# Seven local changes around attention, the output slabs and the embedding gate of a two-layer transformer in one kernel

## The reference, cut to what matters

```python
def hybrid_mixer(u, ...):
    z = u @ w_in                                   # u is rmsnorm(h)
    ...                                            # q, k, v, f_logit: slices of z
    y_attn = forgetting_attention(q, k, v, f_logit) @ w_attn_out
    y_conv = conformer_conv(z[..., C0:GA0], conv_w, conv_b, g_conv) @ w_conv_out
    merged = sigmoid(z[..., GA0:GC0]) * y_attn + sigmoid(z[..., GC0:]) * y_conv
    return merged @ w_out

for i in range(2):
    h = h + 0.5 * swiglu(rmsnorm(h, g_ff1[i]), ...)
    h = h + hybrid_mixer(rmsnorm(h, g_mix[i]), ...)
    h = h + 0.5 * swiglu(rmsnorm(h, g_ff2[i]), ...)
    gate = sigmoid(rmsnorm(h, g_ple[i]) @ w_ple_gate[i])
    h = h + gate * (p[i] @ w_ple_proj[i])
```

## Time and profile before

| | us |
|---|---|
| median of 3 runs | 3079.8 |
| lowest and highest of them | 3076.36, 3082.9 |
| the profiled execution, its own time | 3081.73 |
| its span in the trace | 3079.8 |
| TensorE matmuls busy | 2966.8 (96% of the span) |
| VectorE, ScalarE, GpSimd busy | 2100.2, 1419.6, 483.1 |

### The profile page before, as it was taken

One profiled execution on the slowest core, in us unless ns is written; L12 is line 12 of the kernel. 1 busy time (PEld: TensorE's weight loads), 2 busy tenths in 40 slices (PEclk: granted clock), 3 DMA queues, 4 the chain that ended last, 5 costly groups with the idle time before them and its releaser, 6 DMA issues.

```text
span 3079.8 us, 51785 instructions
## 1 busy us (share of the span) xinstructions
PE 2966.8 (96%) x19012; PEld 2552.3 (83%) x19012; DVE 2100.2 (68%) x3101; ACT 1419.6 (46%) x2295; POOL 483.1 (16%) x392
## 2 busy tenths in 40 slices
PE   7999999999999999999999999999999999999998
PEld 4788888887889988777789987799887777899886
DVE  5666665445599845887699844899547886789535
ACT  3655565443356522334456622566323334466422
POOL 0213223066510011000200012100110000200012
PEclk9999999999999999999999999999999999999998
DMA  6122020223223322222222232223222222233322
GB/s 251 50 53 46 25 66 20 63 79 106 101 84 109 106 91 84 76 69 76 103 94 98 100 110 89 90 101 103 99 86 82 76 69 82 96 109 106 103 97 70
DMA packets 94911, 270.91 MB, mean 88 GB/s; under 512 B 35440, under 2 KB 36592, under 8 KB 93424
## 3 DMA queue, kind: packets, MB, share of 16 engines
q1 hardware_dynamic: 94016, 267.89, 26.3%
q0 software_dynamic: 320, 1.05, 0.1%
q10 hardware_dynamic: 432, 0.02, 0.0%
HBM read 263.68 MB, written 5.24 MB: 87 GB/s over the span
## 4 chain that ended last, share of the span: by engine, by line
PE 83%; DVE 8%; ACT 4%; issue 3%; SPq 2%; DMA 1%; ACTq 0%; DVEq 0%
PE bank L149 15%; PE bank L151 15%; PE bank L150 15%; PE bank L2028 8%; PE bank L2029 8%; PE bank L2030 8%; PE bank L1600 1%; ACT weights_hi L137 1%; SPq L666 1%; DVE weights_lo L142 1%; PE bank L1614 1%; PE bank L1666 1%; PE bank L2526 1%; PE bank L1669 1%; PE bank L2537 1%
## 5 line engine op out<-in xcount | busy, mean ns | idle before, releaser
L142 DVE TENSOR_TENSOR weights_lo<-weights_raw,weights_hi 128x1024 fp32r<-128x1024 f32 (+2 forms) x258 | 393.3, 1524 | 335.3 <-ACT weights_hi L137 331.2
L137 ACT ACTIVATE weights_hi<-weights_raw 128x1024 fp32r<-128x1024 f32 (+2 forms) x250 | 284.9, 1140 | 441.7 <-PE bank L151 433.1
L149 PE MATMUL bank<-x_hi,weights_hi 128*128 128x512 f32 x832 | 338.8, 407 | 9.9 <-DVE x_lo L1916 3.6
L151 PE MATMUL bank<-x_hi,weights_lo 128*128 128x512 f32 x832 | 327.4, 394 | 0.0
L150 PE MATMUL bank<-x_lo,weights_hi 128*128 128x512 f32 x832 | 326.2, 392 | 0.0
L2028 PE MATMUL bank<-sum_hi,block_hi 128*128 128x256 f32 x960 | 272.4, 284 | 3.7 <-ACT bank L2180 3.7
L150 PE MATMUL bank<-hidden_lo,weights_hi 128*128 128x512 f32 x704 | 273.9, 389 | 0.0
L149 PE MATMUL bank<-hidden_hi,weights_hi 128*128 128x512 f32 x704 | 273.9, 389 | 0.0
L151 PE MATMUL bank<-hidden_hi,weights_lo 128*128 128x512 f32 x704 | 273.9, 389 | 0.0
L2029 PE MATMUL bank<-sum_lo,block_hi 128*128 128x256 f32 x960 | 271.9, 283 | 0.0
L2030 PE MATMUL bank<-sum_hi,block_lo 128*128 128x256 f32 x960 | 270.7, 282 | 0.0
(11 more groups left out here) (457 smaller groups left out, 7472.2 us busy)
## 6 DMA issues: line engine op xcount, KB each, us to landing
raw_pair<-w_ff1in SPq DMA_DIRECT2D x42, 1024.0 KB, 4.9
raw_pair<-w_ff2in SPq DMA_DIRECT2D x42, 1024.0 KB, 4.9
weights_raw<-w_mix SPq DMA_DIRECT2D x72, 512.0 KB, 3.3
weights_raw<-w_ff1out SPq DMA_DIRECT2D x32, 704.0 KB, 4.0
weights_raw<-w_ff2out SPq DMA_DIRECT2D x32, 704.0 KB, 4.1
weights_raw<-w_tail SPq DMA_DIRECT2D x42, 512.0 KB, 3.3
mod_weights<-w_mod SPq DMA_DIRECT2D x6, 2048.0 KB, 16.4
weights_raw<-w_dn SPq DMA_DIRECT2D x24, 512.0 KB, 3.5
```

The source lines that it names most:

```text
L137: nc.scalar.activation(K.wh[:, slot, 0:cols], K.raw[:, slot, 0:cols], ACT.Copy).then_inc(S.wh_ready, 1)
L142: nc.vector.tensor_tensor(K.wl[:, slot, 0:cols], K.raw[:, slot, 0:cols], K.wh[:, slot, 0:cols].bitcast(F32), ALU.subtract).then_inc(S.raw_ ...
L149: nc.tensor.matmul(out, K.wh[:, slot, a:b], xh, start=start, stop=False)
L151: return nc.tensor.matmul(out, K.wl[:, slot, a:b], xh, start=False, stop=stop)
```

## The change

1. TensorE writes the first slab of stage c to bank 3 (VectorE reads it there), so that slab 2 finds bank 0 free and waits only for its own weights; slab 3 waits as before.
2. The cumulative forget sum is moved behind the eviction of the first slab of stage at, and that eviction ahead of the `split_lo` of slab 2.
3. `logits(0)` is moved ahead of the four taps that stood before it.
4. ScalarE makes `conved_hi` ahead of the `split_hi` of slab `s1 + 29`, which is the second slab of stage am, and TensorE waits for the convolved tiles one by one.
5. Output slabs 0 and 1 are interleaved: seven K tiles of slab 0, four of slab 1, the last of slab 0, the last four of slab 1.
6. At output slabs 0 to 5 ScalarE and VectorE split the weights of slab m + 2 before they make the parts of x tile m; at slabs 6 and 7 the order stays.
7. The first slab of stage ple goes to banks 4 and 6, and slab 2 no longer waits for its eviction.

```diff
-    def pe_project(pe, s, v, slot, q=None):
+    def pe_project(pe, s, v, slot, bank=None):
...
-            last = mm3(pb[slot][:, :], slot, k, xgh[:, k, :], xgl[:, k, :], k == 0, k == 7)
+            last = mm3(pb[slot if bank is None else bank][:, :], slot, k, xgh[:, k, :], xgl[:, k, :], k == 0, k == 7)
...
-        pe_project(pe, s0, v0, 0)
+        pe_project(pe, s0, v0, 0, 3)
         pe_sum_squares(pe, q)
         pe_project(pe, s0 + 1, v0 + 1, 1)
-        with pe.Fori(1, 4) as i:
+        pe_project(pe, s0 + 2, v0 + 1, 0)
+        pe_project(pe, s0 + 3, v0 + 3, 1)
+        with pe.Fori(2, 4) as i:
...
-            if first:
-                pe.wait_ge(S.cv_ready, 4 * (l + 1))
             for k in range(4):
+                if first:
+                    pe.wait_ge(S.cv_ready, 4 * l + k + 1)
                 last = mm3(pb[2 + slot][:, :], slot, 4 + k, K.cv_h[:, k, :], K.cv_l[:, k, :], k == 0, k == 3)
...
-        wo(0, 0, True)
-        wo(1, 1, False)
+        pe.wait_ge(S.raw_read, s4 + 1 + CREDIT)
+        pe.wait_ge(S.evac, v4 + 1)
+        for k in range(7):
+            pe.wait_ge(S.mg_ready, 8 * l + k + 1)
+            wo_tile(0, k)
+        pe.wait_ge(S.raw_read, s4 + 2 + CREDIT)
+        pe.wait_ge(S.evac, v4 + 2)
+        for k in range(4):
+            wo_tile(1, k)
+        pe.wait_ge(S.mg_ready, 8 * l + 8)
+        wo_tile(0, 7).then_inc(S.slab_done, 1)
+        for k in range(4, 8):
+            last = wo_tile(1, k)
+        last.then_inc(S.slab_done, 1)
...
-        split_hi(act, s1 + 29, 1, 1024)
         for t in range(4):
             act.wait_ge(S.cs_ready, 4 * l + t + 1)
             nc.scalar.activation(K.cv_h[:, t, :], K.cy[:, t, :], ACT.Copy).then_inc(S.cvh_ready, 1)
+        split_hi(act, s1 + 29, 1, 1024)
...
-        with act.Fori(0, 4) as i:
+        with act.Fori(0, 3) as i:
             for slot in range(2):
                 m = 2 * i + slot
+                split_hi(act, s4 + m + 2, slot, 1024)
                 act_gain(act, q + 1, m, v4 + m)
-                split_hi(act, s4 + m + 2, slot, 1024)
                 plain_x(act, q + 1, m)
...
-            nc.vector.tensor_tensor(K.glu[:, i, 30:542], pb[0][:, :], rstd[:, :], ALU.mult).then_inc(S.evac, 1)
+            nc.vector.tensor_tensor(K.glu[:, i, 30:542], pb[3 if first else 0][:, :], rstd[:, :], ALU.mult).then_inc(S.evac, 1)
...
+        dve.wait_ge(S.slab_done, s1 + 1 + CREDIT)
+        mixed_out(0)
+        dve.wait_ge(S.fln_ready, l + 1)
...
+        split_lo(dve, s1 + 2, 0, 1024)
         taps(4)
         slab_out(1)
         taps(4)
         slab_out(2)
+        logits(0)
         taps(4)
-        logits(0)
...
-        with dve.Fori(0, 4) as i:
+        with dve.Fori(0, 3) as i:
...
+                split_lo(dve, s4 + m + 2, slot, 1024)
                 dve_gain(dve, q + 1, m)
-                split_lo(dve, s4 + m + 2, slot, 1024)
...
-        tile(0, 0, True)
+
+        tile(0, 0, True, at=4)
         pe_sum_squares(pe, q)
         tile(1, 1, False)
-        with pe.Fori(1, 4) as i:
+        tile(2, 0, False, v0 + 2)
+        tile(3, 1, False)
+        with pe.Fori(2, 4) as i:
```

More of the change, by code:

```diff
@@ L2601, in mix_pe, with wo_tile, wo @@
         s4, v4 = K.slab(l, "wo"), K.evic(l, "wo")
-        def wo(m, slot, first):
+        def wo_tile(slot, k):
+            return mm3(pb[slot][:, :], slot, k, K.mg_h[:, k, :], K.mg_l[:, k, :], k == 0, k == 7)
+        def wo(m, slot):
             pe.wait_ge(S.raw_read, s4 + m + 1 + CREDIT)
@@ L2606, in wo @@
             for k in range(8):
-                if first:
-                    pe.wait_ge(S.mg_ready, 8 * l + k + 1)
-                last = mm3(pb[slot][:, :], slot, k, K.mg_h[:, k, :], K.mg_l[:, k, :], k == 0, k == 7)
+                last = wo_tile(slot, k)
             last.then_inc(S.slab_done, 1)
-        wo(0, 0, True)
-        wo(1, 1, False)
+        pe.wait_ge(S.raw_read, s4 + 1 + CREDIT)
[12 more added lines that the diff above has]
+        last.then_inc(S.slab_done, 1)
         with pe.Fori(1, 4) as i:
             for slot in range(2):
-                wo(2 * i + slot, slot, False)
+                wo(2 * i + slot, slot)
     def mix_act(act, l):
@@ L2727, in mix_act @@
         s4, v4 = K.slab(l, "wo"), K.evic(l, "wo")
-        with act.Fori(0, 4) as i:
+        with act.Fori(0, 3) as i:
             for slot in range(2):
                 m = 2 * i + slot
+                split_hi(act, s4 + m + 2, slot, 1024)
                 act_gain(act, q + 1, m, v4 + m)
-                split_hi(act, s4 + m + 2, slot, 1024)
                 plain_x(act, q + 1, m)
+        for m in (6, 7):
+            act_gain(act, q + 1, m, v4 + m)
+            split_hi(act, s4 + m + 2, m % 2, 1024)
+            plain_x(act, q + 1, m)
     def mix_dve(dve, l):
@@ L2787, in mix_dve, with mixed_out @@
             glu(i, False)
[L2788 to L2794, removed]
         s1, v1 = K.slab(l, "at"), K.evic(l, "at")
-        def slab_out(t):
-            split_lo(dve, s1 + t + 2, t % 2, 1024)
+        def mixed_out(t):
             kind, i = mixer_slab(t)
@@ L2809, in slab_out @@
             ins.then_inc(S.evac, 1)
+        def slab_out(t):
+            split_lo(dve, s1 + t + 2, t % 2, 1024)
+            mixed_out(t)
         def logits(n):
@@ L2833, in attended @@
                 .then_inc(S.ao_ready, 1)
-        slab_out(0)
+        dve.wait_ge(S.slab_done, s1 + 1 + CREDIT)
+        mixed_out(0)
+        dve.wait_ge(S.fln_ready, l + 1)
+        chain.link(nc.vector.tensor_tensor(K.fx[R, :], K.fx[R, :], K.fe[R, :], ALU.subtract))
+        chain.link(nc.vector.tensor_tensor_scan(K.fc[R, :], K.onerow[R, :], K.fx[R, :], 0.0, ALU.mult, ALU.add))
+        chain.link(nc.vector.tensor_copy(K.fch[R, :], K.fc[R, :]))
+        nc.vector.tensor_tensor(K.fcl[R, :], K.fc[R, :], K.fch[R, :].bitcast(F32), ALU.subtract).then_inc(S.cm_ready, 1)
+        chain.leave(LAYERS, FCHAIN)
+        hold(dve, S)
+        split_lo(dve, s1 + 2, 0, 1024)
         taps(4)
@@ L2895, in mix_dve @@
                 nc.vector.tensor_tensor(h[:, m, :], pb[slot][:, :], h[:, m, :], ALU.add).then_inc(S.evac, 1)
+                split_lo(dve, s4 + m + 2, slot, 1024)
                 dve_gain(dve, q + 1, m)
-                split_lo(dve, s4 + m + 2, slot, 1024)
+        for m in (6, 7):
+            dve.wait_ge(S.slab_done, s4 + m + 1 + CREDIT)
+            nc.vector.tensor_tensor(h[:, m, :], pb[m % 2][:, :], h[:, m, :], ALU.add).then_inc(S.evac, 1)
+            dve_gain(dve, q + 1, m)
+            split_lo(dve, s4 + m + 2, m % 2, 1024)
     def mix_pool(pool, l):
@@ L2927, in ple_pe, with tile @@
         s0, v0 = K.slab(l, "ple"), K.evic(l, "ple")
-        def tile(m, slot, first):
+        def tile(m, slot, first, freed=None, at=0):
             pe.wait_ge(S.raw_read, s0 + m + 1 + CREDIT)
-            pe.wait_ge(S.evac, v0 + m + 1)
+            pe.wait_ge(S.evac, v0 + m + 1 if freed is None else freed)
             if first:
@@ L3008, in tile @@
                 dve_rstd(dve, q, v0)
-            scaled(m, slot)
-            gated(m, slot)
+            scaled(m, slot, 4 if first else 0)
+            gated(m, slot, 4 if first else 0)
         tile(0, 0, True)
```

14 lines of the change are left out of this document (6 added, 8 removed).

## The result

The changed kernel took 3059.15 us (median of 4 runs, 3055.95 to 3059.49) beside 3081.1 us for the kernel before (4 runs): a ratio of 0.9929, 95% interval 0.9912 to 0.9946. That is 22 us less where 18.5 were forecast; the time lies inside the range of 3055 to 3068. The profiled execution took 3058.96 us, with a span of 3057.0.

A forecast was written before the change was run, and what follows sets the result against it. TensorE, busy nearly the whole span, was taken as the bound, so its stops set the gain. Layers' 7.5 and 7.8 us gave 15.3, plus 3.2 for the clock: 18.5, so 3061.3 against the median; range 3055 to 3068.

The forecast's parts named there:

- Edit 5's net of 1.34: Output slabs: interleaving with weights first removes a 2.26 us wait but adds 0.92 at slab 2, per layer.
- the squares get ahead of `weights_lo` of slab 2: Output slab 2: GpSimd's squares start at 1505.15, just ahead of `weights_lo`, which waits and ends at 1507.3.
- wait 0.52 for 0.65: Output slab 2: TensorE was forecast to stop 0.65 us for its weights, 0.92 charged with the restart.
- The third rival's counter-argument: Against new waits at output slab 2 and am (4.9 us less gain, chance 0.12): GpSimd's work starts after VectorE's weights request.
- The x part was taken at 0.7: Output slabs: VectorE's x part assumed as long as `h`, 0.7 us, in a slab total of 5.5 beside 5.4.
- the smaller of two numbers: Convolved tiles and stage am: TensorE's wait frees 1.81 us, the earlier merge loop 1.70; 1.70 was taken.
- 2.19 forecast: Stage ple, slab 2: the wait for the eviction vanishes, 1.92 + 0.27 = 2.19 us per layer.
- 0.70 for 0.60: Attention slab 2: with the forget sum moved, TensorE was forecast to go 0.60 us earlier, not the whole 1.11.
- 0.65 for 0.44: First turn: with `logits` ahead of the taps, `probs` was forecast to start 0.44 us earlier, about 1.5 of wait staying.
- the prediction moved `probs` by 0.32: First turn: `probs` starts when the taps end, moved by 0.28 of `logits` and its read-out, to about 1267.56.
- Two stretches of half rate: Layer 2, behind `merged_lo` and in ple: half-rate clock goes with the vanishing waits, 2 x 1.6 = 3.2 us.
- the one behind `probs` I leave, since 1.5 us of its wait stays: Behind `probs` of layer 1: the half-rate stretch was expected to remain, so no gain was counted.

The follow-up runs named there:

- squares_later: Changed kernel with GpSimd's squares of output slabs 0 to 5 held until the weights of slab m + 2 are split; output slabs 43.61 / 43.63 us, not 44.4.
- gain_first: Changed kernel with x tile parts again ahead of the weights at all output slabs, interleaving kept; output slabs took 46.24 / 46.30 us.
- tiles_only: Changed kernel with ScalarE's old order of `weights_hi` ahead of `conved_hi`, TensorE's tile by tile waits kept; first am to first output matmul 47.83 us.
- act_only: Changed kernel with TensorE waiting for all four convolved tiles at once, ScalarE's new order kept; first am to first output matmul 46.01 / 46.02 us.
- no_interleave: Changed kernel with output slabs 0 and 1 one after the other, weights still split first; output slabs 45.70 us in layer 1, 47.32 in layer 2.
- no_ple: Changed kernel with the bank change of stage ple undone; second feed-forward output to last slab matmul of layer 2 took 178.69 us, not 174.79.
- weights_before_sigmoids: Changed kernel with ScalarE making the weights ahead of the sigmoids in stage am; first am to first output matmul 43.52 us in both layers.

## Why the prediction was right, and where its sizes were off

**Edits 1, 4, 5 with 6, and 7** came within 0.2 us a layer of their terms. Edit 5's net of 1.34 rested on one step that could have gone either way, that the squares get ahead of `weights_lo` of slab 2: it went as worked out (wait 0.52 for 0.65; `weights_lo` 1.97 long), squares_later shows that it was GpSimd, and gain_first that without edit 6 nothing would be left. The third rival's counter-argument, that each unit of GpSimd's work starts after VectorE's request, doesn't fit this working: the squares stood 0.10 ahead in it and stand 0.15 ahead in the trace. The x part was taken at 0.7 and takes 1.77 at ten of 16 slabs (0.75 before), since it now starts while `square_sum` runs; it still ends inside the 5.4 us of a slab, so that this cost nothing.

**Edit 4** was said to be worth the smaller of two numbers, TensorE's wait and what the loop of merges gains by an earlier `gates`. tiles_only shows the first freed and nothing won, act_only the second alone and all of it won. `gates` starts 3.60 us behind the first am matmul, and not 5.43, which is where 1.8 rather than 1.7 comes from.

**Edit 7** gave 2.2 in layer 2 (2.19 forecast) and 2.0 in layer 1, for the longer wait at the first x tiles shown above; the prediction charged nothing there.

**Edit 2** gave 0.70 for 0.60: TensorE started 0.05 us behind the end of `weights_lo`, where it had started 0.15 behind `queries`.

**Edit 3** gave 0.65 for 0.44. The term that was mis-sized is what `logits` costs when it stands first. In the changed kernel:

```profile
1263.54 0.28 DVE L2836 CUSTOM_DVE_ANT_0 logits<-forget_rows,bank 128x128 f32<-128x128 f32 x1
1263.74 0.08 DVE L2836 DVE_READ_ACCUMULATOR2_ANT negmax<- 128x1 f32 x1
1263.74 2.73 DVE L2775 SCALAR_TENSOR_TENSOR conv_out<-glu,conv_taps,conv_out 128x512 f32<-128x512 f32 x4
1266.39 0.15 DVE L2842 RECIPROCAL rowinv<-rowsum 128x1 f32<-128x1 f32 x1
```

The taps start 0.20 behind the start of `logits`, where the prediction moved `probs` by 0.32 for it (1267.24 to 1267.56), and `probs` starts 2.65 behind the start of the taps, not 2.73: operations of VectorE overlap by 0.08 at a seam, which I had charged in full. Together 0.20 of the 0.21.

**The clock.** Two stretches of half rate were forecast to go with their waits, and they did (the output slabs and ple of layer 2, 3.2 us; no_interleave and no_ple bring one back each, 1.6 us). One step failed, "the one behind `probs` I leave, since 1.5 us of its wait stays": it went too, 1.52 us. That three stretches were there to lose is shown by both profiles of the kernel before; that two of them were `merged_lo` and ple of layer 2 was read from one execution, and the second has `merged_lo` of both layers and `probs` of layer 2. Nine profiles have the shortened wait of 1.35 us in both layers, 18 cases, and none is followed by half rate. The waits of 1.9 to 2.4 us at the same places (two profiles of the kernel before, gain_first, no_interleave, no_ple) are 18 cases too, and eight are.

**The whole difference.** Of the 22.8 us between the two spans the waits are 16.2 (1.28 + 1.29, 1.40, 1.30, 3.63, 1.37 + 1.7, and 2.0 + 2.2 for edit 7), 15.3 forecast, and the three stretches above 4.7. Another 2.5 us lie between the last output matmul of layer 1 and layer 2, where edit 7 explains 2.0 of 4.48: the traces show 16 matmuls at half rate at each of two feed-forward entries before and none after (squares_later, with one such stretch, takes 758.20 for this way and weights_before_sigmoids, with none, 757.42: 0.8 each), and by difference 0.9 more at the x tiles of layer 2's first stage. In the other direction the untouched first part cost 1.0 more. The last 0.4 are 0.2 between the first `attend` and the first am matmul of layer 2 (135.75 in both profiles of the kernel before, 135.56 after) and 0.2 behind the last slab matmul.

**What stays open.** Whether the change makes half rate rarer at the feed-forward entries. TensorE's waits there (0.9, 1.1 and 1.9 us) are the same in all kernels and no edit touches them, yet five of six entries behind the first attention have it in the two profiles of the kernel before, and 10 of 33 in the eleven of the changed kernel and its variants, the changed kernel's own at layer 2's second among them. And the untouched first part took 1186.7 to 1196.1 us over all profiles, about as much as the runs of one kernel differ. It goes with the clock: before that landmark TensorE's granted clock stood at half for 10 and 17 us in the two shortest cases (1187.4, 1186.7), for 31 us in each of the three longest (1195.7 to 1196.1), and for 20 to 27 us in the eight between. What makes the clock fall more often in one execution than in another no run here shows. Edits 1, 2 and 3 were not undone singly; their gains are read from the landmarks and the rows behind them. How near the total came to the forecast is in part luck: 18.5 stands beside 22 in one comparison and 24.5 in the other.

## What to carry to other kernels

Where one engine is busy 96% of the time, list its stops, ask for each what ends it and what would end it next, and charge a removed wait its bracket plus the restart; six terms of 0.4 to 2.2 us then add up to a forecast within a few us. Look behind each wait too, at the clock: a wait of 2 us may cost 1.6 us more. Don't read a gain of a few us off two spans, since the first part alone, which no edit touches, moved by 9.4 us. And follow what the freed engine needs next: the interleaved slabs halved the time for the next weights, and one edit was worth nothing without the other.

## What the runs showed of the hardware

- The same wait of about 2 us was followed by TensorE at half rate in eight of 18 cases, at other places in two profiles of one and the same kernel; a wait of 1.35 us in none of 18. Eight matmuls of 512 columns then cost 1.6 us more.
- VectorE's subtraction of two SBUF tiles (`weights_lo`, output slabs) took 1.97 to 2.31 us in the 166 cases of 13 profiles where it started with 0.9 us or more of a GpSimd instruction still to run, and ended 1.08 or 1.09 us behind that instruction. It took 1.22 or 1.23 when it met none. In the 14 cases where it started first it took 1.21, and GpSimd's squares 1.77 for 1.04. The addition of a PSUM tile to `h`, with one SBUF input, took 0.68 or 0.69, also in the four cases of squares_later where GpSimd was at work.
- The first 1190 us of this program, which no edit touches, took 1186.7 to 1196.1 us in 13 profiles; TensorE's granted clock stood at half for 10 and 17 us of it in the two shortest and for 31 us in the three longest. The layers' stages up to the output slabs, where no half rate came in, repeated to 0.06 us.
